# Gate/up by seven block products, with the sums on VectorE

## What is computed

```
def rmsnorm(x, g):
    y = x * lax.rsqrt(jnp.mean(x * x, axis=-1, keepdims=True) + NORM_EPS)
    return y * g

    x = x + mix @ w_out[l]
    h = rmsnorm(x, norm_ffn_g[l])
    gate, up = jnp.split(h @ w_gate_up[l], 2, axis=-1)
    x = x + (jax.nn.silu(gate) * up) @ w_down[l]
return rmsnorm(x, norm_final_g)
```

## Time and profile before

| | us |
|---|---|
| median of 3 runs (1453.48 to 1453.53) | 1453.52 |
| the profiled execution, own time | 1455.37 |
| its span | 1453.6 |
| TensorE busy in the span | 1383.6 |
| VectorE busy | 664.4 |
| ScalarE busy | 386.3 |
| GpSimd busy | 43.8 |

### The profile page before, as it was taken

How to read it: one execution, slowest core, us unless ns; L and a number is a source line. 1 busy time by engine, 2 the same in 40 slices (tenths; PEclk the granted TensorE clock), 3 DMA queues, 4 the chain that set the end, 5 groups by cost and what they waited for, 6 DMA issues and landing times.

```text
span 1453.6 us, 18955 instructions
## 1 busy us (share of the span) xinstructions
PE 1383.6 (95%) x7441; PEld 1153.1 (79%) x7441; DVE 664.4 (46%) x1011; ACT 386.3 (27%) x717; POOL 43.8 (3%) x57
## 2 busy tenths in 40 slices
PE   7999999888599999899999999999999999999994
PEld 6888887565599999788888888888888887888784
DVE  6644423787587777554443232243323242323333
ACT  6001232676123322332322111121111121112113
POOL 0000000112000100100000000000000000000000
PEclk9999999999899999899999999999999999999997
DMA  5111221000212222411011111111111111211112
GB/s 217 43 48 43 80 96 65 23 1 23 56 49 79 63 50 55 183 44 44 30 58 58 33 45 67 44 43 51 44 51 58 44 33 46 67 44 51 29 51 115
DMA packets 57132, 84.41 MB, mean 58 GB/s; under 512 B 19952, under 2 KB 36336, under 8 KB 56816
## 3 DMA queue, kind: packets, MB, share of 16 engines
q1 hardware_dynamic: 57072, 83.58, 18.0%
HBM read 69.37 MB, written 13.64 MB: 57 GB/s over the span
## 4 chain that ended last, share of the span: by engine, by line
PE 89%; ACT 4%; DVE 4%; DMA 1%; issue 1%; ACTq 0%; SPq 0%; DVEq 0%
PE bank L330 64%; PE bank L1248 4%; PE bank L344 3%; PE bank L1278 2%; PE bank L435 2%; ACT scores L969 2%; PE bank L1348 1%; DVE scores L1001 1%; PE bank L1342 1%; PE bank L1255 1%; PE bank L1390 1%; PE bank L869 1%; PE bank L881 1%; PE bank L1360 1%; PE bank L1377 1%
## 5 line engine op out<-in xcount | busy, mean ns | idle before, releaser
L309 DVE TENSOR_TENSOR ring_wlo<-ring_raw,ring_whi 128x1024 fp32r<-128x1024 f32 (+2 forms) x102 | 114.3, 1121 | 504.6 <-ACT ring_whi L303 504.6
L330 PE MATMUL bank<-x1hi,ring_whi 128*128 128x512 f32 x688 | 268.0, 389 | 0.2 <-DVE ring_wlo L309 0.2
L330 PE MATMUL bank<-x1hi,ring_wlo 128*128 128x512 f32 x688 | 267.7, 389 | 0.0
L330 PE MATMUL bank<-x1lo,ring_whi 128*128 128x512 f32 x688 | 267.6, 389 | 0.0
L303 ACT ACTIVATE ring_whi<-ring_raw 128x1024 fp32r<-128x1024 f32 (+2 forms) x102 | 99.1, 972 | 525.6 <-PE bank L330 503.1
L330 PEld LDWEIGHTS bank<-x1hi,ring_whi 128*128 128x128 f32 x688 | 129.1, 188 | 27.4 <-issue 0.6
L330 PEld LDWEIGHTS bank<-x1lo,ring_whi 128*128 128x128 f32 x688 | 129.2, 188 | 26.9
L330 PEld LDWEIGHTS bank<-x1hi,ring_wlo 128*128 128x128 f32 x688 | 129.1, 188 | 26.6
L330 PE MATMUL bank<-hidhi,ring_whi 128*128 128x512 f32 x308 | 120.0, 390 | 0.0
L330 PE MATMUL bank<-hidlo,ring_whi 128*128 128x512 f32 x308 | 119.9, 389 | 0.0
L330 PE MATMUL bank<-hidhi,ring_wlo 128*128 128x512 f32 x308 | 119.8, 389 | 0.0
(11 more groups left out here) (266 smaller groups left out, 1973.0 us busy)
## 6 DMA issues: line engine op xcount, KB each, us to landing
ring_raw<-in_w_gate_up SPq DMA_DIRECT2D x44, 512.0 KB, 3.4
ring_raw<-in_w_in SPq DMA_DIRECT2D x20, 512.0 KB, 3.5
ring_raw<-in_w_down SPq DMA_DIRECT2D x16, 384.0 KB, 3.1
ring_raw<-in_w_down SPq DMA_DIRECT2D x16, 320.0 KB, 2.9
xin<-in_x_t SPq DMA_DIRECT2D x8, 512.0 KB, 8.9
n_scratch<-NB SPq DMA_DIRECT2D x8, 512.0 KB, 3.2
XT<-inv_scratch SPq DMA_DIRECT2D x8, 512.0 KB, 4.0
x<-in_x_t SPq DMA_DIRECT2D x2, 2048.0 KB, 8.5
```

The costliest lines, as they stand in the source:

```text
L309: dve.tensor_tensor(self.ring.lo[:, s, 0:self.kt, :], self.ring.raw[:, s, 0:self.kt, :], self.ring.hi[:, s, 0:self.kt, :].bitcast(F32), AL ...
L330: mm = pe.matmul(o[:, :], wpart[:, s, k, :], apart[:, k, c], start=i == 0, stop=i == n - 1)
```

## The change

Let the tokens be halved (low and high half of 512) and the 1024 input channels be halved (four k tiles each). For a hidden tile the kernel needs gate and up over both token halves, a 2 x 2 block result from 2 x 2 blocks of weights (gate, up by channel half) and 2 x 2 blocks of activations. The change computes it, for 20 of the 22 tiles, by the seven products of the Winograd form of Strassen's method. Each product is 4 k tiles x 3 passes = 12 matmuls into one bank.

- The first two tiles (`PLAIN = 2`) stay as they were, as one `Layer` (`GUC`). `PAIRS = 20` tiles follow in an unrolled loop; a pair is the gate and the up tile of one hidden tile.
- Three banks hold a tile's results: X (p1 then p2 on top), Y (p6, p7 on top, p4 on top) and Z (p5, p3 on top). Between two products on one bank VectorE or ScalarE reads the partial sum. TensorE's order is p6, p5, p2, p7, p3, p1 of the next tile, p4. Banks alternate between tiles.
- The four sums of weight blocks (`sums`) and all sums of results are made by VectorE. ScalarE copies p1 and p5 out of their banks. Every weight block or sum is split into high and low parts in a slot of its own (`ahi`, `alo`), which is refilled when its product is done.
- The four sums of activation blocks are made once, in `x1`, after it is scaled by the norm's gain in place: `block_sums` and one more subtraction, of which most stand in stage 6 ahead of the norm's reciprocal. Their split parts (`thi`, `tlo`) fill the place where `mhi` and `mlo` were. So that `x1` can be overwritten, each of its k tiles is first stored to memory (`x1_scratch`) in stage 6 and is read back after the last pair.
- `up` is no longer multiplied by `rsb2`; that scale is applied to the down layer's product (`add` is now a multiply and an add). `gat` and `hid` have two buffers.
- Hidden tiles are stored to memory (`hid_scratch`) and come back for the down layer, which now runs as a whole behind all gate/up tiles, in groups of 6, 8 and 8.

The diff, cut to its core:

```diff
-GROUPS = [6, 6, 5, 5]
+GROUPS = [6, 8, 8]
+PLAIN = 2
+PAIRS = FF // P - PLAIN
...
+    x_dram = nc.dram_tensor("x1_scratch", (P, KD, T), F32, kind="Internal").ap()
+    h_dram = nc.dram_tensor("hid_scratch", (FF // P, P, T), F32, kind="Internal").ap()
...
+        def block_sums(dve, k0, k1):
+
+            a, b = x1[:, k0:k1, 0:HALF], x1[:, k0:k1, HALF:T]
+            c, d = x1[:, 4 + k0:4 + k1, 0:HALF], x1[:, 4 + k0:4 + k1, HALF:T]
+            dve.wait_ge(s_xscale, 4 + k1)
+            dve.tensor_tensor(b, d, b, ALU.subtract).then_inc(s_tb, 1)
+            dve.tensor_tensor(d, d, a, ALU.subtract).then_inc(s_tb, 1)
+            dve.wait_ge(s_tb, 6 if k0 else 3)
+            dve.tensor_tensor(c, c, d, ALU.subtract).then_inc(s_tb, 1)
...
+            for s in range(2):
+                OUT.load(sp, s, 1, 2 + s)
+            for k in range(KD):
+                s = k % 2
+                if k + 4 < KD:
+                    OUT.load(sp, s, (k + 4) // 2, k + 4)
+                elif k + 4 < KD + 2:
+                    GUC.load(sp, s, 0, s * FF // P)
+                sp.wait_ge(s_x1, 2 * k + 2)
+                sp.dma_start(x_dram[:, k, :], x1[:, k, :]).then_inc(s_xs[k], 16)
...
+            def scaled(k):
+                act.wait_ge(s_xs[k], 16)
+                act.wait_ge(s_x1lo, k + 1)
+                act.activation(x1[:, k, :], x1[:, k, :], ACT.Copy, scale=par[:, R_N2 + k:R_N2 + k + 1]).then_inc(s_xscale, 1)
...
+            scaled(KD - 2)
+            OUT.J.result(act, "11", OUT.n - 1)
+            moved_high(act, 1, 1, x1[:, 0:4, 0:HALF])
+            scaled(KD - 1)
...
+            dve.wait_ge(s_xscale, 4)
+            dve.tensor_tensor(x1[:, 0:4, 0:HALF], x1[:, 0:4, HALF:T], x1[:, 0:4, 0:HALF], ALU.subtract).then_inc(s_tb, 1)
+            dve.wait_ge(s_tb, 1)
+            block_sums(dve, 0, 3)
+            moved_low(dve, 1, 1, x1[:, 0:4, 0:HALF])
             N2.emptied(dve, "col", 0)
...
+            block_sums(dve, 3, 4)
...
+                sp.wait_ge(s_alo, place["p4", n] + 1)
+                if n + 2 < PAIRS:
+                    load(n + 2)
+                elif n + 1 < PAIRS:
                     for s in range(2):
...
+                        DN0.load(sp, s, 0, s, rows=0)
+                if n:
+                    spill(n - 1 + PLAIN)
+                if n + 1 == PAIRS:
+                    for f in range(3):
+                        land_hidden(f)
+            for f in range(3, GROUPS[0]):
+                land_hidden(f)
+            V.result(sp, "Y", PAIRS - 1)
+            for k in range(KD - 1):
+                sp.dma_start(x1[:, k, :], x_dram[:, k, :]).then_inc(s_xr2[k // 4], 16)
+            spill(PAIRS - 1 + PLAIN)
+            sp.wait_ge(s_hl7, GROUPS[0])
+            sp.dma_start(x1[:, KD - 1, :], x_dram[:, KD - 1, :]).then_inc(s_xr2[1], 16)
+            for gi, layer in enumerate(DN):
+                more = gi + 1 < len(DN)
+                for turn in range(KD // 2):
                     for s in range(2):
...
+                        if turn + 1 < KD // 2:
+                            layer.load(sp, s, turn + 1, 2 * (turn + 1) + s, rows=first_of[gi])
+                        elif more:
+                            DN[gi + 1].load(sp, s, 0, s, rows=first_of[gi + 1])
                     if more:
+                        f = first_of[gi + 1]
+                        if gi == 0 and turn == 0:
+                            spilled(sp, FF // P - 1)
+                        for i in range(2 * turn + 2 if turn else 0, min(2 * turn + 4, GROUPS[gi + 1])):
+                            land_hidden(f + i)
...
+            moved_high(act, 0, 6, x1[:, 4:8, HALF:T])
+            for half in range(2):
+                silu(0, half)
+            GUC.split_hi(act, 0, 1)
+            moved_high(act, 2, 5, x1[:, 0:4, HALF:T])
+            GUC.split_hi(act, 1, 1)
+            moved_high(act, 3, 7, x1[:, 4:8, 0:HALF])
+            for half in range(2):
+                silu(1, half)
+            for j in ("p1", "p6", "p5", "p2", "p7", "p3"):
+                high(j, 0)
...
+            for n in range(PAIRS):
+                more = n + 1 < PAIRS
+                if more:
+                    high("p6", n + 1)
+                else:
+                    DN0.split_hi(act, 0, 0)
+                    hidden_high(0)
+                    hidden_high(1)
+                product_done(act, "p5", n)
+                if n:
+                    act.wait_ge(s_c22, n)
+                act.activation(p5, V.bank("Z", n)[:, :], ACT.Copy).then_inc(s_p5, 1)
+                if more:
+                    high("p5", n + 1)
+                    high("p2", n + 1)
+                else:
+                    hidden_high(2)
+                    DN0.split_hi(act, 1, 0)
+                silu(n + PLAIN, 0)
+                if more:
+                    high("p7", n + 1)
+                    high("p3", n + 1)
+                    keep_p1(n + 1)
+                else:
+                    hidden_high(3)
+                silu(n + PLAIN, 1)
+                if more:
+                    if n + 2 < PAIRS:
+                        high("p1", n + 2)
+                    high("p4", n + 1)
+                else:
+                    hidden_high(4)
+                    hidden_high(5)
...
+            for n in range(PAIRS):
+                f, more = n + PLAIN, n + 1 < PAIRS
+                h = hid_of(f)
+                x, y, z = (V.bank(name, n)[:, :] for name in ("X", "Y", "Z"))
+                product_done(dve, "p6", n)
+                dve.wait_ge(s_p1, n + 1)
+                dve.wait_ge(s_sil, 2 * f)
+                dve.tensor_tensor(gat[1][:, :], y, p1[n % 2], ALU.add).then_inc(s_u2, 1)
+                low("p4", n)
+                if more:
+                    low("p6", n + 1)
+                    sums(n + 1, True)
+                else:
+                    DN0.split_lo(dve, 0, 0)
+                    hidden_low(0)
+                product_done(dve, "p2", n)
+                V.read(dve.tensor_tensor(gat[0][:, :], x, rsb2[:, lows], ALU.mult), "X", n)
+                V.emptied(dve, "X", n)
+                dve.sem_inc(s_gat, 1)
+                if more:
+                    low("p5", n + 1)
+                else:
+                    hidden_low(1)
+                product_done(dve, "p7", n)
+                if f > PLAIN:
+                    spilled(dve, f - 2)
+                dve.tensor_tensor(h[:, highs], y, p1[n % 2], ALU.add).then_inc(s_u3, 1)
+                if more:
+                    low("p2", n + 1)
+                dve.wait_ge(s_u3, n + 1)
+                dve.wait_ge(s_p5, n + 1)
+                dve.tensor_tensor(h[:, highs], h[:, highs], p5, ALU.add).then_inc(s_c22, 1)
+                if not more:
+                    hidden_low(2)
+                product_done(dve, "p3", n)
+                dve.wait_ge(s_u2, n + 1)
+                V.read(dve.tensor_tensor(gat[1][:, :], z, gat[1][:, :], ALU.add), "Z", n)
+                if more:
+                    low("p7", n + 1)
+                V.emptied(dve, "Z", n)
+                dve.tensor_tensor(gat[1][:, :], gat[1][:, :], rsb2[:, highs], ALU.mult).then_inc(s_gat, 1)
+                if more:
+                    low("p3", n + 1)
+                else:
+                    spilled(dve, f - 1)
+                    DN0.split_lo(dve, 1, 0)
+                    hidden_low(3)
+                if n + 2 < PAIRS:
+                    sums(n + 2, False)
+                product_done(dve, "p4", n)
+                V.read(dve.tensor_tensor(h[:, lows], y, p1[n % 2], ALU.add), "Y", n)
+                dve.wait_ge(s_sil, 2 * f + 2)
+                dve.wait_ge(s_c22, n + 1)
+                dve.tensor_tensor(h[:, highs], h[:, highs], sil[:, highs], ALU.mult).then_inc(s_hidb, 1)
+                V.emptied(dve, "Y", n)
+                dve.tensor_tensor(h[:, lows], h[:, lows], sil[:, lows], ALU.mult).then_inc(s_hida, 1)
+                if n + 2 < PAIRS:
+                    low("p1", n + 2)
+                elif not more:
+                    hidden_low(4)
+                    hidden_low(5)
...
+            def add(layer, s, turn):
+                for half in range(2):
+                    b = layer.J.result(dve, f"{s}{half}", turn)
+                    c = slice(half * HALF, (half + 1) * HALF)
+                    v, tmp = x1[:, 2 * turn + s, c], gat[half][:, :]
+                    layer.J.read(dve.tensor_tensor(tmp, b[:, :], rsb2[:, c], ALU.mult), f"{s}{half}")
+                    layer.J.emptied(dve, f"{s}{half}", turn)
+                    ins = dve.tensor_tensor(v, tmp, v, ALU.add)
+                    ins.then_inc(s_added, 1)
+
+            for gi in range(len(DN)):
+                last = gi + 1 == len(DN)
+                for turn in range(KD // 2):
+                    layer = down(gi, turn)
+                    if not last:
+                        for i in range(2 * turn, 2 * turn + 2):
+                            hidden_low(first_of[gi + 1] + i)
```

(42 more changed lines are left out.)

388 lines of the change are left out of this document (252 added, 136 removed).

## The result

The changed kernel takes 1412.13 us in the median of four runs (1410.76 to 1413.41), beside 1453.53 us for the kernel before. The ratio is 0.971, with a 95% interval of 0.9694 to 0.9727: faster by 41.4 us, where 44.2 were forecast. Its profiled execution is the run of 1412.85 us, with a span of 1411.0.

What follows compares the result with a forecast made beforehand. TensorE's gapless matmul stream was taken as the bound: -54.4 (240 matmuls) - 3.0 (old waits) + 2.4 + 1.5 + 6.0 + 2.4 + 0.9 = -44.2 us, from 1453.5 to 1409.3; this case spans 1404 to 1415, the overall range 1400 to 1425.

Steps and rivals of the forecast that it cites:

- The pair loop at nothing: In the gate/up loop, VectorE's 13.8 us fit within TensorE's 19.04 us an iteration, so the loop costs nothing extra.
- Entry: Entering the layer, the new block sums and their splits delay TensorE's second turn: 2.4 us, from 0.5 to 4.
- Leaving the loop: In the last iteration, ScalarE's high splits of hidden tiles 0 and 1 delay p5's copy: 1.5 us, 0 to 3.5.
- The reload of x1: After the first down turn, TensorE waits for weights split after hidden tiles queued behind the x1 reload: 6 us.
- The clock after it: After the 6 us wait at the down layer, TensorE runs 12 matmuls at half clock: 2.4 us, 0 to 3.
- The end: At the kernel's end, the last add becomes a multiply, a wait for the bank's release and an add: 0.9 us.
- B: Rival for the joints: all are covered, as transfers are faster or TensorE has its weights; 1399.4 us, chance 0.15.
- C: Rival for the reload of x1: it runs at 247 GB/s, with waits of 3.5 and 15.5 us; 1420.8 us, chance 0.20.
- D: Rival for the pair loop: hand-overs cost 0.5 to 1 us an iteration; 1419 to 1429 us, chance 0.12.
- E: Rival for the stream: fewer matmuls but no shorter, because waits fill it; within 0.2%, chance 0.02.
- F: Slower rival for the pair loop: VectorE's serial chain bounds it, deciding from 21.25 us an iteration; 1468 at 22, chance 0.04.
- G: Slower rival for the loop: bank changes every 12 matmuls leave gaps and the clock falls; a third makes 1521, chance 0.02.

Runs made afterwards that it cites:

- spill_first: Changed kernel with the last hidden tile's store sent ahead of the reload of x1 on SP's queue: 1413.28 us.
- x1_last: Changed kernel with the reload of x1 sent after hidden tiles 6 and 7 are asked for, and VectorE's wait for it moved behind the weights' split: 1401.90 us.
- vector_plus4: Changed kernel with four more VectorE additions of 448 columns in each loop iteration: 1411.43 us.
- vector_plus9us: Changed kernel with twelve more VectorE additions (880, 512 and 512 columns ahead of each of four waits) in each loop iteration: 1457.43 us.
- combined2: Changed kernel with x1_last's order at the first down turn, and the last iteration and entry reordered as in combined: 1405.25 us.
- combined: Changed kernel with second-turn weights before hidden tiles, p5 copied first, hidden tiles' low splits behind the wanted sums, and silu before the block sum on entry: 1406.07 us.
- two_pass: Changed kernel with the third pass of every product in the loop left out, 56 matmuls an iteration: 1293.27 us.

## Why the prediction was right

The mechanism, the sign and nearly every term held. One of the prediction's own signs of being wrong did come, though: a wait over 10 us at the down layer. It was 10.8 us in this execution, though not in the others with the same joint.

- **Matmuls removed.** 54.4 us, shown by the kernel with 258 fewer (58.4 measured for 58.5) and by the spacing in the loop, 0.2269 us.
- **The pair loop at nothing.** Right: one wait of 0.2 us in 380 us of loop. The hand schedule is visible in VectorE's five waits; the smallest is for p6's result, which the schedule had 0.2 us late and the trace has 0.2 us early. Its six operations before p4 left 1.7 us, where I had counted 1.1, since neighbouring operations start 0.60 us apart and not 0.69. TensorE had its 1680 matmuls of the seven products.
- **Entry.** 2.0 us for 2.4: the wait of the diagonal scalings was 0.3 for 0.5, and the chain through the block sum's high split, the table load, silu and the weights was as written. ScalarE's timeline shows it:

```profile
719.10 1.91 ACT L1647 ACTIVATE thi<-x 128x2048 fp32r<-128x2048 f32 x1
721.02 1.28 ACT L1928 ACT_TABLE_LOAD   x1
722.32 1.16 ACT L1928 ACTIVATE sil<-gat 128x512 f32<-128x512 f32 x2
723.38 1.04 ACT L317 ACTIVATE ring_whi<-ring_raw 128x1024 fp32r<-128x1024 f32 x1
```

- **Leaving the loop.** 1.6 us for 1.5.
- **The reload of x1.** The one mis-sized term: 10.8 us for 6, inside its bounds of 4 and 15.5. The step that failed is the landing of the reload and of what stands behind it. Counted from the last product's end, the last of the seven x1 tiles landed at 14.3 us and not at 8.8, the store at 16.0 and not at 12.5 (14.1 with the 1.6 us that I added), and tile 6 at 22.6 and not at 16. Two things were left out. SP needed 4.6 us to send the seven, 0.33 to 1.41 us for each. And the eighth x1 tile and two weight tiles, 1.3 MB, were ahead of tile 6, which took 6.5 us and not 3.5. The rate was not far off the 415 GB/s assumed once the queue was full: the windows from 1135 to 1145 moved 395 and 353 GB/s, but from 1130 to 1135 it was 270. Other kernels with the same joint had 7.7 to 8.9 us for the same wait, so up to some 3 us of the miss of 4.8 is what this chain varies by. In this trace the transfers land in the order in which they were sent, and spill_first shows the same: moving the store ahead took 8.3 us off it and laid 5.5 on the load. The Trainium skill, "DMA: Bandwidth & Descriptors", section "Queues, rings and completion order", says that each DMA engine consumes an issuing engine's descriptors in order. Both traces agree.
- **The clock after it.** 2.5 us for 2.4. The prediction took short waits to be free of this (it speaks of three in the kernel before; rows 3 has four). That held here, for waits of 1.6 and 1.7 us, but not in every kernel: x1_last lost 1.6 us of time to it behind a wait of 2.0.
- **The end.** 0.5 us for 0.9: the multiply and the wait for the bank cost less than I counted.
- **Rivals.** B (all joints covered, 1399.4) and C (1420.8) were the ends, and the truth lies between forecast and C. D, E and F are refuted by the loop's waits and by vector_plus4, in which 3.9 us of VectorE's slack are still left in each iteration; F's deciding point of 21.25 us was met from the other side by vector_plus9us. G did not come: the granted clock is 1.00 through the loop, though banks are taken up again after every 12 matmuls, and even with gaps (275 of 300 us busy in vector_plus9us) it stayed. The rule of the Trainium skill, "TensorE: Matmul & The Clock Gate", section "A second HAM failure mode: psum-queue depth-cycling", speaks of short idles between groups of matmuls. The changed kernel's loop has cycled banks but none of these idles, and vector_plus9us, which has them, kept its clock at 1.00.

The median moved by 41.4 us and the forecast was 44.2. The miss of 4.8 us at the reload is partly offset by the entry and the end (0.4 each), and two small terms were 0.1 higher each, so that the terms as measured give 40.0. That the median is 1.4 us nearer to the forecast than they are is luck: the kernels' runs spread by some 3 us. The prediction's span for this case, 1404 to 1415 "with the bounds of each term", is narrower than its bounds, which give 1401.5 to 1423 when all fall to one side.

## What to carry to other kernels

When an engine's stream has no gaps, an algorithm that removes part of it pays count times spacing, and the work is to find where the new feeding chains surface, which is at the joints and not in the steady loop. For each joint, write down all that stands ahead of the wanted transfer on the issuing queue, in its program order and in bytes, and give each link the landing time of a loaded queue (here 10 to 13 us for 512 KB, where one alone takes 3 to 4). A reordering that takes one wait away must be followed through the issuing engine's program too, since by its trace that is where combined2 lost what it had gained.

## What was unexpected of the hardware

- A store of 512 KB lands after a median of 6.2 us in this kernel, after 11.3 us behind 3.7 MB of loads, and after 3.0 us when it goes first (spill_first). SP's issues of the seven loads took 0.66 us each on average, where 0.33 to 0.43 is what the first ones took; why isn't shown.
- After 10.8 us without matmuls TensorE needed until about 1162 to 1165 us to be back at full clock, 2.5 us lost.
- The length of a short wait does not tell whether the clock falls. It stayed at 1.00 after waits of 1.6 and 1.7 us, in a loop with gaps over 8% of the time, and after 3.1 us in combined (for the 3.5 us behind it); it fell after 2.8 us in two_pass and after 2.0 us in x1_last. What decides between these isn't shown.
- VectorE can be kept 97.7% busy (195.3 of 200 us in two_pass) with five hand-overs from TensorE in each 12.69 us, without holding TensorE up in that stretch.
